# The delta rule's level steps done per value head, and the dense blocks dealt out anew among the steps of a trip

## The reference, cut to what matters

```python
m = jnp.where(strict, beta[..., :, None] * kk * decay, 0.0) + jnp.eye(C, dtype=f32)
rhs = jnp.concatenate([v * beta[..., None], k * (beta * jnp.exp(gc))[..., None]], axis=-1)
sol = lax.linalg.triangular_solve(m, rhs, left_side=True, lower=True, unit_diagonal=True)
...
def step(state, inp):
    u = u0_c - jnp.einsum("bhcd,bhde->bhce", w_c, state)
    o = jnp.einsum("bhcd,bhde->bhce", qd_c, state) + jnp.einsum("bhcj,bhje->bhce", qk_c, u)
    state = cd_c[..., None, None] * state + jnp.einsum("bhcd,bhce->bhde", kd_c, u)
```

## Time and profile before

| what | value |
|---|---|
| median of 3 runs | 4023.48 us (4019.49 to 4024.85) |
| profiled execution, its time | 4022.14 us |
| its span in the trace | 4020.4 us |
| PE busy | 3476.5 us (86%) |
| PE weight loads busy | 2835.5 us (71%) |
| DVE busy | 1887.5 us (47%) |
| ACT busy | 744.3 us (19%) |
| POOL busy | 1832.9 us (46%) |
| mean granted PE clock | 0.94 of full speed |

### The profile page before, as it was taken

How to read it: one execution, slowest core, us unless ns; L and a number is a source line. 1 busy time by engine, 2 the same in 40 slices (tenths; PEclk the granted TensorE clock), 3 DMA queues, 4 the chain that set the end, 5 groups by cost and what they waited for, 6 DMA issues and landing times.

```text
span 4020.4 us, 46841 instructions
## 1 busy us (share of the span) xinstructions
PE 3476.5 (86%) x17070; PEld 2835.5 (71%) x17070; DVE 1887.5 (47%) x2385; ACT 744.3 (19%) x974; POOL 1832.9 (46%) x1828
## 2 busy tenths in 40 slices
PE   7789988888888888888858999799998888859897
PEld 6567777776777777777747778587777666648675
DVE  2422356556547655655653221434445655541333
ACT  3411122112212221211221010111112222230111
POOL 5445633323423332342322567466665444416574
PEclk9899999999999999999979999899999999979998
DMA  4322211111101111111121322222221111122222
GB/s 160 126 79 84 89 48 63 52 42 63 63 35 48 63 52 42 63 58 36 52 78 63 146 87 101 95 100 94 94 94 71 65 57 65 65 106 101 84 84 83
DMA packets 53363, 306.68 MB, mean 76 GB/s; under 512 B 5012, under 2 KB 7188, under 8 KB 21812
## 3 DMA queue, kind: packets, MB, share of 16 engines
q1 hardware_dynamic: 33984, 247.48, 17.7%
q10 hardware_dynamic: 19316, 58.32, 3.9%
HBM read 284.74 MB, written 21.04 MB: 76 GB/s over the span
## 4 chain that ended last, share of the span: by engine, by line
PE 60%; DVE 29%; issue 4%; ACT 4%; DMA 1%; POOL 1%; DVEq 0%; ACTq 0%; SPq 0%; POOLq 0%
DVE arena L739 23%; PE gemm_ps L369 15%; PE gemm_ps L370 15%; PE gemm_ps L371 15%; DVE arena L745 5%; PE bankA L486 3%; PE bankC L498 2%; ACT arena L1369 2%; PE bankB L496 2%; PE bankA L645 1%; POOL w_lo L327 1%; PE bankB L511 1%; DVE a_lo L739 1%; ACT L1369 1%; PE bankA L505 1%
## 5 line engine op out<-in xcount | busy, mean ns | idle before, releaser
L369 PE MATMUL gemm_ps<-a_hi,w_hi 128*128 128x512 f32 (+1 forms) x3744 | 1542.1, 412 | 166.3 <-DVE a_lo L739 86.8
L342 POOL CAST w_hi<-w_raw 128x512 fp32r<-128x512 f32 x880 | 559.6, 678 | 2091.4 <-issue 2075.3
L370 PE MATMUL gemm_ps<-a_lo,w_hi 128*128 128x512 f32 (+1 forms) x3744 | 1470.6, 393 | 0.0
L371 PE MATMUL gemm_ps<-a_hi,w_lo 128*128 128x512 f32 (+1 forms) x3744 | 1468.1, 392 | 0.0
L327 POOL TENSOR_TENSOR w_lo<-w_raw,w_hi 128x512 fp32r<-128x512 f32 x944 | 1281.2, 1387 | 53.5 <-ACT w_hi L1369 53.5
L369 PEld LDWEIGHTS gemm_ps<-a_hi,w_hi 128*128 128x128 f32 x3744 | 730.9, 195 | 338.6 <-issue 134.1
L371 PEld LDWEIGHTS gemm_ps<-a_hi,w_lo 128*128 128x128 f32 x3744 | 726.9, 194 | 149.7
L370 PEld LDWEIGHTS gemm_ps<-a_lo,w_hi 128*128 128x128 f32 x3744 | 730.8, 195 | 136.1 <-issue 12.8
L739 DVE TENSOR_TENSOR arena<-gemm_ps,arena 128x512 f32<-128x512 f32 (+3 forms) x234 | 157.6, 674 | 1048.7 <-PE gemm_ps L371 1001.3
L1369 ACT ACTIVATE arena<-arena 128x512 f32<-128x512 f32 (+4 forms) x345 | 233.2, 676 | 1091.0 <-DVE arena L739 1069.5
L739 DVE TENSOR_TENSOR arena<-arena 128x256 f32<-128x256 f32 (+4 forms) x432 | 330.8, 766 | 79.6 <-ACT arena L1595 43.6
(11 more groups left out here) (130 smaller groups left out, 1939.8 us busy)
## 6 DMA issues: line engine op xcount, KB each, us to landing
w_raw<-w_stream SPq DMA_DIRECT2D x236, 1024.0 KB, 4.8
y_scratch<-arena ACTq DMA_DIRECT2D x20, 512.0 KB, 6.5
arena<-y_scratch ACTq DMA_DIRECT2D x15, 512.0 KB, 3.6
arena<-gc_scratch ACTq DMA_DIRECT2D x12, 512.0 KB, 3.6
arena<-x_t ACTq DMA_DIRECT2D x1, 4096.0 KB, 15.1
arena<-y_scratch ACTq DMA_DIRECT2D x1, 4096.0 KB, 25.2
x_scratch<-arena ACTq DMA_DIRECT2D x1, 4096.0 KB, 13.3
y_out<-arena ACTq DMA_DIRECT2D x4, 1024.0 KB, 3.9
```

Source lines behind the costliest of these rows:

```text
L342: pool.tensor_copy(part(w_hi, w, q), part(w_raw, w, q)).then_inc(pool_step, 1)
L369: pe.matmul(o, hi, a_hi[:, k, 0:width], start=(k == 0), stop=False)
L370: pe.matmul(o, hi, a_lo[:, k, 0:width], start=False, stop=False)
L371: last = pe.matmul(o, lo, a_hi[:, k, 0:width], start=False, stop=(k == KT - 1))
```

## The change

A level's `half` and `whole` become two steps each, one for each value head a: four products and a copy of 512 columns on ACT in a `half`, eight products and two predicated copies of 512 columns on DVE in a `whole`. In the list the order within a level is `half` a = 0, `half` a = 1, `whole` 0, `whole` 1. Semaphores count per head (`level_count`). The numbers behind the steps change, and the run behind the loop gets numbers of its own. Line numbers behind the top of the file grow by 9 to 13 (L739 becomes L752, L745 L758, L1369 L1381, L486 L499).

```diff
-DN_STEPS = ([("qk_norm", 36), ("natural", 6), ("transposed", 5)]
-            + [(s, l, g) for l in range(1, LEVELS) for s, g in (("half", 2), ("whole", 4))]
-            + [(s, n, g) for n in range(NB) for s, g in (("rest", 2), ("update", 1.5), ("output", 2))]
-            + [("head_out", 5)])
+def dn_steps(norm, level):
+    return ([("qk_norm", norm), ("natural", 7), ("transposed", 7)]
+            + [(s, l, a, level) for l in range(1, LEVELS) for s in ("half", "whole") for a in range(2)]
+            + [(s, n, g) for n in range(NB) for s, g in (("rest", 2.2), ("update", 1.8), ("output", 2.25))]
+            + [("head_out", 6)])
+DN_STEPS = dn_steps(39, 0.5)
+DN_END_STEPS = dn_steps(30, 0.875)
...
+        def level_count(j, l, a):
+            return 2 * ((LEVELS - 1) * j + l - 1) + a + 1
...
                 elif step[0] == "half":
-                    pe.wait_ge(s["x_ready"], j + 1)
-                    if step[1] > 1:
-                        pe.wait_ge(s["lvl"], (LEVELS - 1) * j + step[1] - 1)
+                    l, a = step[1:3]
+                    if l > 1:
+                        pe.wait_ge(s["lvl"], level_count(j, l - 1, a))
                     else:
+                        pe.wait_ge(s["x_ready"], j + 1)
                         pe.wait_ge(s["nT_sbuf"], j + 1)
-                    for a in range(2):
-                        for n in range(NB):
-                            last = pe.matmul(quad(bankA)[:, a, n, :], NmT[:, a, n, :], X[:, a, n, :],
-                                             start=True, stop=True)
+                    for n in range(NB):
+                        last = pe.matmul(quad(bankA)[:, a, n, :], NmT[:, a, n, :], X[:, a, n, :],
+                                         start=True, stop=True)
...
-            for step in interleave(EARLY, DN_STEPS):
+            for step in interleave(EARLY, DN_END_STEPS):
...
-                elif step[0] == "half" and step[1] == 2:
+                elif step[0] == "half" and step[1:3] == (2, 1):
...
-                    v.wait_ge(s["dd"], (LEVELS - 1) * j + step[1])
-                    if step[1] < LEVELS - 1:
-                        copy_after(v.copy_predicated, X[:, :, :, :].rearrange(flat),
-                                   low[:, step[1]:step[1] + 1, :].to_broadcast([P, 8, P]), quad(bankB).rearrange(flat))
+                    l, a = step[1:3]
+                    v.wait_ge(s["dd"], level_count(j, l, a))
+                    if l < LEVELS - 1:
+                        copy_after(v.copy_predicated, X[:, a, :, :], low[:, l:l + 1, :].to_broadcast([P, NB, P]),
+                                   quad(bankB)[:, a, :, :])
...
-                    act.wait_ge(s["t1"], (LEVELS - 1) * j + step[1])
-                    op(T1[:, :, :, :], quad(bankA), ACT.Copy, s["t1_sbuf"], (LEVELS - 1) * j + step[1])
+                    l, a = step[1:3]
+                    act.wait_ge(s["t1"], level_count(j, l, a))
+                    op(T1[:, a, :, :], quad(bankA)[:, a, :, :], ACT.Copy, s["t1_sbuf"], level_count(j, l, a))
```

More of the change, by code:

```diff
@@ L478, in dn_mix @@
                 elif step[0] == "half":
[L479 to L481 removed]
+                    l, a = step[1:3]
+                    if l > 1:
+                        pe.wait_ge(s["lvl"], level_count(j, l - 1, a))
                     else:
+                        pe.wait_ge(s["x_ready"], j + 1)
                         pe.wait_ge(s["nT_sbuf"], j + 1)
[L484 to L487 removed]
+                    for n in range(NB):
+                        last = pe.matmul(quad(bankA)[:, a, n, :], NmT[:, a, n, :], X[:, a, n, :],
+                                         start=True, stop=True)
                     last.then_inc(s["t1"], 1)
                 elif step[0] == "whole":
[L490 to L491 removed]
+                    l, a = step[1:3]
+                    pe.wait_ge(s["t1_sbuf"], level_count(j, l, a))
+                    if l == 1:
                         pe.wait_ge(s["kd_ready"], j + 1)
[L493 to L499 removed]
+                    for n in range(NB):
+                        if l < LEVELS - 1:
+                            pe.matmul(quad(bankB)[:, a, n, :], XT[:, a, n, :], T1[:, a, n, :],
+                                      start=True, stop=True)
+                        last = pe.matmul(quad(bankC)[:, a, n, :], T1[:, a, n, :], XT[:, a, n, :],
+                                         start=True, stop=True)
                     last.then_inc(s["dd"], 1)
@@ L1804 @@
             + [("values", 0)])
-DN_VECTOR_STEPS = 74
+DN_VECTOR_STEPS = 79
 def kernel(**inputs):
```

17 lines of the change are left out of this document (4 added, 13 removed).

## The result

| kernel | median us | range of its runs |
|---|---|---|
| before | 4021.99 | 4019.49 to 4024.85, 4 runs |
| after | 4098.05 | 4095.32 to 4100.7, 4 runs |

The changed kernel is slower: the ratio is 1.0189, with a 95% interval of 1.0171 to 1.0206, so 76 us. That is far outside the noise; whether it is more than 2% the interval leaves open. The profiled execution of after took 4095.32 us.

The account below looks back on a forecast made before the run. A trip was taken as a closed circle of DVE's fixed 36.5 us and PE's half from gate to `head_out`. That half's +6.6 us made +73 in eleven trips; the last trip's -8 left +65 on 4023.5: 4088 us, range 4045 to 4122.

Parts of the forecast that it names:

- first half, `head_out` to gate: DVE's way from `head_out` to tile 2's first block: stays 36.5 us, since the change touches none of that work.
- wait at the gate: PE's wait at tile 2's first block: 7.8 us in place of 5.3, since `natural` no longer fills it.
- wait ahead of `whole` 1: PE waits 7.9 us there for ACT's copies, queued behind the SiLU of tile 2.
- tile 3: Ends between the halves of level 6: PE waits 4.4 us for convolution, SiLU and copy.
- tile 4: Ends ahead of `update` 2: PE waits 4.9 us for convolution, SiLU and copy.
- level borders: PE waits 0.5 us for predicated copies at each of five borders between levels, 2.5 us a trip.
- second half, change: Gate to `head_out`: +6.6 us a trip, from waits +5.7, moved blocks and `natural` +1.9, holes -1.0.
- last trip: Trip without SiLU and convolution: 8 us less (4 to 12), from an earlier residual load and fewer waits.
- ACT's queue holds the levels: The forecast itself, chance 0.70: SiLUs queued ahead of ACT's level copies hold PE; 4088 us, own range 4060 to 4115.
- Rival 3: Faster, chance 0.11: the SiLU costs PE nothing as ACT reaches the copies in time; 3965 us.
- the holes: PE's gaps beside ACT copies, which one block did not cover, go: -1.0 us a trip (0 to -2).
- the even clock: Time at PE's lower clock taken as unchanged by the change, with bounds of -1.9 to +3.9 us a trip.

Follow-up runs that it names:

- e1: After, with ACT's SiLUs of tiles 2, 3 and 4 issued later, behind `half` 2, `half` 6 and `update` 2: 3972.43 us.
- e5: Before, with 48 semaphore increments that nobody reads added to DVE's loop, eight per level: 4064.45 us in one run.
- e3: After, with ten DVE instructions of the loop's body folded into others (`kd` scalings, beta scalings in `rest`): 4060.88 us.
- e7: After, with the edits of e1 and e3, convolution taps issued one at a time behind following steps, and SiLUs moved further back to match: 3834.46 us.
- e9: e7 with `natural` put back to block 32, ahead of the gate, and the freed blocks given to the levels: 3800.61 us.
- e10: Before, levels not split and its own numbers, with folded DVE instructions as in e3, spread taps as in e7 and late SiLUs: 3873.39 us.
- e11: e7 with the levels split and the step numbers of before, tile 3's SiLU one chunk earlier: 3816.67 us.
- e4: After with the numbers behind the steps of before, also behind the loop: the split without the new spread, 4013.17 us.

## Why the prediction was right, and where it was not

The forecast was 4088 us, the median is 4098: inside the range, and slower by the mechanism that had the chance of 0.70. But two errors of opposite sign stand behind it. By its own steps, per trip:

| step | predicted | measured |
|---|---|---|
| first half, `head_out` to gate | 36.5 | 41.6 |
| wait at the gate | 7.8 | 12.4 |
| wait ahead of `whole` 1 | 7.9 | 6.8 |
| tile 3 | 4.4 | 3.7 |
| tile 4 | 4.9 | 4.6 |
| level borders | 2.5 | 1.2 |
| second half, change | +6.6 | +3.3 |
| low clock (on work) | as before, 18.4 (15.1) | 28.3 (16.5) |
| last trip | -8 | -13.7 |

**Shown: ACT's queue holds the levels.** The three waits are where the prediction put them, on ACT. e1 takes the hold away and nothing else, and 10 us a trip go, three times the rise of the second half (3.3). Rival 3, that the SiLU costs PE nothing, is out by its own sign: the SiLU of tile 2 starts at 1608.35, 5.4 us after `half` 1.

**The step that failed: "this half stays 36.5 us whatever PE has to fill it with".** The reason given, that the change touches none of DVE's work there, is true: DVE is busy for 32.64 us of it before and after. What the step left out is that the change lengthens DVE's loop elsewhere: eleven predicated copies more, and the waits and counts that go with them, 272 records a trip for 239. The first instruction behind the jump back waits 5.4 us, with two packets of the instruction queue inside. e5 makes this wait without the change, e3 takes it from the changed kernel and leaves the rest, and the gate's wait is then 7.1 us, near the 7.8 of the prediction. The prediction named a DVE later than 36.5 us as something that would prove it wrong, and in this step it is: 10 x 5.1 = 51 us that it did not see. The kernel nearest to the one forecast, with a first half of 36.6 us, is e3 (ten DVE operations fewer), and it took 4060.88 us, 27 under the forecast.

**Mis-sized: the waits, 19.7 predicted and 16.3 measured.** The longest is off by the convolution. The prediction took 6.2 us from the earlier trace rows; at its new place it is 1608.32 - 1604.20 = 4.1 us. PE was also ready 0.5 us sooner than thought (22.6 behind the gate, not 23.1), and ACT 1.6 us sooner (1609.72 - 1580.36 = 29.4, not 31.0). The level borders came at half their price. The same half in the trip of before, as one stretch:

```profile
817.48:922.10 104.62, 90.09 (x523) 76.79 (x524) 52.78 (x72) 15.36 (x20) 26.29 (x24) 0.92 0.12 41
```

PE's idle time in it rose from 104.62 - 90.09 = 14.5 to 108.29 - 92.02 = 16.3 us, where +4.7 (5.7 less the holes) had been forecast, and its busy time by 1.9 us, which is what the moved `natural` less two blocks was to cost. That agreement is this trip's: over the eleven second halves PE's busy time grew by 1.4 us (90.6 to 91.9) and its idle time by 2.0.

**Even in cost, not in time: the clock.** The time at the lower clock rose by 9.9 us a trip, from 18.4 to 28.3. (The prediction's 17 us leave out the stretch from 863.10 to 892.80; its trip had 20.5.) But only 15.1 of it fell on PE's work before and 16.5 after; the rest lies in waits, where it costs nothing. At half speed the difference is 0.7 us a trip, 8 us in eleven. So the even clock was nearly right in what it cost. In the trip shown the low stretches stand where the prediction put them, at the gate and at the three waits on ACT (from 1573.3, 1607.5, 1655.2 and 1675.7 us); they are longer, and what is longer lies in the waits. The bound of +3.9 was not reached in after. The waits on ACT did have a price in clock: e1, without them, has 9.9 us a trip on work, and e7, e9, e10 and e11 have 4 to 5. The Trainium skill ("TensorE: Matmul & The Clock Gate", HAM oscillation) says that such a loss is the throttled time times 1 - 1.2 / 2.4; from after to e9 that is 11 x 21.7 / 2 = 119 us at most, and the loop's PE busy time fell by 1337.67 - 1267.96 = 70 us. The trace agrees once the time on work alone is counted, 11 x (16.5 - 5.1) / 2 = 63 us. The row of e9's loop:

```profile
506.20:1853.40 1347.20, 1267.96 (x7394) 1089.27 (x7395) 925.11 (x1156) 312.00 (x441) 516.16 (x523) 0.97 0.17 60
```

**The last trip** gave back 13.7 us, not 8. Its listed waits, those on `a_lo` left out, 13.9 us before (the 9.4 of the earlier trace rows and 4.5 smaller ones), are 9.1 us now; PE is busy for 5.7 us less outside the loop (2134.8 to 2129.1). e4 parts it by cause: 3.3 us come with the split (1961.4 to 1958.1) and 10.5 with the new list behind the loop (to 1947.6), each from one execution.

In sum: the ten fetches and eleven second halves make 10 x 5.1 + 11 x 3.3 = 87 us where 11 x 6.6 = 73 were forecast, and the last trip -13.7 where it was -8: 73 us in place of 65. What the fetch added, the overpriced second half and the last trip mostly took back; so near a hit does not speak for the terms.

## What to carry to other kernels

When an order of steps is shared by all engines, look on each engine at what stands ahead of the small urgent copies: an operation whose operand comes late (here a SiLU of 0.63 us behind a convolution) holds everything behind it in that queue, and moving three of them back was worth 126 us. Count the instructions of an engine's loop before making steps finer: past some length (here between 263 and 271 records on DVE) each turn of the loop waits for code, which shows as an idle time put down to "issue" ahead of the body's first instruction and as more packets in the instruction queue. And measure parts of such a change apart: here the split (worth 5 us a trip) was good, its cost in code ate it, and the new numbers of the loop that came with it cost 8 us a trip on top (e4 to after), and still 2.7 with both queues mended (e11 to e7). Look also at where a low clock falls before pricing it: most of what after has more of it lies in waits.

## What the runs showed of the hardware

- **Code of a loop.** DVE's body of 263 trace records was kept, bodies of 271, 272 and 287 were fetched anew in the ten turns of the loop, at 4.3 to 5.5 us of idle time a turn and five packets (about 8 KB each, 0.42 MB / 51).
- **DVE beside POOL.** Three `scalar_tensor_tensor` of 128x512 with both operands in SBUF took 2.33 us at 1605.99 and 4.35 us at 843.96. Their single durations in ns (min/median/max), after and then before:

```profile
L752 DVE SCALAR_TENSOR_TENSOR arena<-arena x3: 751/751/752, 1606.0 to 1607.6; 128x512 f32<-128x512 f32 x3
```

```profile
L739 DVE SCALAR_TENSOR_TENSOR arena<-arena x3: 975/1641/1667, 844.0 to 846.6; 128x512 f32<-128x512 f32 x3
```

  POOL's rows of the same two places, after (before DVE's three start) and then before (while they run):

```profile
L340 POOL TENSOR_TENSOR w_lo<-w_raw,w_hi x3: 1261/1265/1268, 1602.0 to 1604.4; 128x512 fp32r<-128x512 f32 x3
```

```profile
L327 POOL TENSOR_TENSOR w_lo<-w_raw,w_hi x3: 1705/1735/1738, 844.4 to 847.7; 128x512 fp32r<-128x512 f32 x3
```

  In the first case POOL had ended at 1605.67; in the second it ran throughout. DVE's first one at 843.96 started beside a POOL `CAST` and took 0.98 us; the other two ran beside POOL's `TENSOR_TENSOR` and took 1.64 and 1.67, where one alone takes 0.75. POOL's own went from 1.27 to 1.74 us. That is the error in the convolution above. The Trainium skill ("SBUF — State Buffer", SBUF: two separate sides) says that a VectorE operation with two inputs in SBUF and a GpSimd one that reads SBUF lock each other out for whole instructions. The trace agrees that each delays the other and that the price hangs on POOL's operation; but a pair takes 1.7 us, less than the 0.75 + 1.27 = 2.0 that two durations end to end would make.
